# First block's attention logits as three fp32r part products, their maxima bank by bank, and the heads' loads at other tiles

## The reference

```
q = concat(q_nope, rope(q_rope))              # 96 per head
k = concat(k_nope, rope(k_rope))              # the 32 rope columns are shared by all heads
logits = einsum('bqhd,bkhd->bhqk', q, k) * (1 / sqrt(96))
p = softmax(logits, axis=-1)
o = einsum('bhqk,bkhd->bqhd', p, v)
```

## Time and profile before

| | |
|---|---|
| median of 3 runs | 2934.79 us (2934.61 to 2935.14) |
| the profiled execution | 2935.57 us, span 2934.2 us |
| TensorE busy | 2836.1 us (97%) |
| VectorE, ScalarE, GpSimd busy | 1356.9, 1125.4, 1277.9 us |
| heads of c0 | 91.0 to 151.8 us |
| heads of l0 | 288.1 to 406.8 us |
| heads of l1 | 1128.1 to 1246.8 us |
| modulation weights, 512 KB each | 6.5 us from issue to landing (median) |

### The profile page before, as it was taken

One profiled execution on the slowest core, in us unless ns is written; L12 is line 12 of the kernel. 1 busy time (PEld: TensorE's weight loads), 2 busy tenths in 40 slices (PEclk: granted clock), 3 DMA queues, 4 the chain that ended last, 5 costly groups with the idle time before them and its releaser, 6 DMA issues.

```text
span 2934.2 us, 40890 instructions
## 1 busy us (share of the span) xinstructions
PE 2836.1 (97%) x16278; PEld 2341.0 (80%) x16278; DVE 1356.9 (46%) x2527; ACT 1125.4 (38%) x1917; POOL 1277.9 (44%) x828
## 2 busy tenths in 40 slices
PE   7789999999999999989999899999999999999999
PEld 6577778888888786778888787888878878888887
DVE  5448643241211576632211457776542368667432
ACT  4353554553332444543332344332433344323332
POOL 4253247874444442344444353343534433435343
PEclk9899999999999999999999999999999999999999
DMA  7834114653233324033333222111223221212222
GB/s 260 307 106 152 39 49 151 181 160 101 94 94 129 113 82 144 1 108 94 96 93 102 71 97 69 58 58 58 87 72 94 77 89 49 68 58 72 85 73 87
DMA packets 81981, 291.67 MB, mean 99 GB/s; under 512 B 9216, under 2 KB 9600, under 8 KB 81408
## 3 DMA queue, kind: packets, MB, share of 16 engines
q1 hardware_dynamic: 81792, 289.06, 30.6%
HBM read 286.93 MB, written 2.10 MB: 99 GB/s over the span
## 4 chain that ended last, share of the span: by engine, by line
PE 84%; DVE 10%; ACT 2%; issue 2%; POOL 1%; DMA 1%; SPq 0%; POOLq 0%; ACTq 0%; DVEq 0%
PE ps L625 65%; PE ps L598 5%; DVE ps L2263 4%; PE ps L769 3%; PE ps L790 2%; PE ps L958 1%; PE ps L653 1%; PE ps L1021 1%; PE ps L1032 1%; PE ps L894 1%; PE ps L1199 1%; DVE t L2555 1%; DVE t L2593 1%; POOL t L2895 1%; PE ps L907 0%
## 5 line engine op out<-in xcount | busy, mean ns | idle before, releaser
L625 PE MATMUL ps<-t,t 128*128 128x512 f32 (+3 forms) x9936 | 2210.7, 380 | 20.9 <-DVE t L2027 7.4
L625 PEld LDWEIGHTS ps<-t,t 128*128 128x128 f32 x9936 | 1778.5, 189 | 366.5 <-issue 33.1
L2895 POOL TENSOR_TENSOR t<-t,t 128x1024 fp32r<-128x1024 f32 (+3 forms) x444 | 1041.0, 2348 | 1105.4 <-ACT t L1335 1064.9
L1335 ACT ACTIVATE t<-t 128x1024 fp32r<-128x1024 f32 (+3 forms) x444 | 457.9, 1035 | 855.1 <-PE ps L625 806.0
L598 PE MATMUL ps<-t,t 128*128 128x128 f32 (+2 forms) x1662 | 237.5, 279 | 33.9 <-DVE t L2078 12.2
L598 PEld LDWEIGHTS ps<-t,t 128*128 128x128 f32 (+2 forms) x1662 | 190.4, 141 | 80.9 <-ACT t L1448 16.1
L2366 DVE TENSOR_TENSOR ps<-ps,t 128x512 f32<-128x512 f32 (+1 forms) x96 | 57.2, 606 | 344.1 <-ACT t L1641 344.1
L2379 DVE TENSOR_TENSOR t<-ps,t 128x512 f32<-128x512 f32 x60 | 40.9, 692 | 217.6 <-PE ps L625 217.5
L2263 DVE SCALAR_TENSOR_TENSOR ps<-t,t,ps 128x512 f32<-128x512 f32 (+1 forms) x174 | 116.1, 667 | 6.4 <-ACT ps L1556 0.6
L2915 POOL TENSOR_TENSOR t<-t,t 128x4 f32<-128x4 f32 (+2 forms) x93 | 85.6, 921 | 75.3 <-DVE t L2036 39.3
L769 PE MATMUL ps<-t,t 96*128 96x384 f32 (+1 forms) x320 | 105.6, 453 | 4.8 <-DVE t L2126 2.4
(11 more groups left out here) (264 smaller groups left out, 2398.8 us busy)
## 6 DMA issues: line engine op xcount, KB each, us to landing
t<-in_wbig SPq DMA_DIRECT2D x412, 512.0 KB, 3.5
t<-in_wmod SPq DMA_DIRECT2D x96, 512.0 KB, 6.5
t<-in_wbig SPq DMA_DIRECT2D x16, 416.0 KB, 3.2
t<-in_wbig SPq DMA_DIRECT2D x14, 256.0 KB, 2.7
t<-in_wbig SPq DMA_DIRECT2D x8, 332.0 KB, 3.0
t<-in_wbig SPq DMA_DIRECT2D x6, 384.0 KB, 3.1
t<-in_x SPq DMA_DIRECT2D x1, 2048.0 KB, 8.2
out<-t SPq DMA_DIRECT2D x8, 256.0 KB, 2.1
```

The costliest lines, as they stand in the source:

```text
L625: m = p.matmul(out, lhs, rhs, start=kk == 0 and n == 0, stop=kk == tiles - 1 and n == 2)
L1335: a.activation(c.hi(w), c.raw(w), ACT.Copy).then_inc(w_hi.h, w_hi.up(("cut", w)))
L2895: g.tensor_tensor(c.lo(w), c.raw(w), c.hi(w).bitcast(F32), ALU.subtract).then_inc(w_lo.h, w_lo.up(("cut", w)))
```

## The change

Queries and keys of a head are held as a high part (fp32r, written by ScalarE) and a low part (written by VectorE as the difference). The logits are three fp32r products per bank. For the context tokens all 256 keys go to one bank; the latent stages' low parts lie in AH and AL. VectorE takes the maximum of each bank by itself. `load_head` moves from the second to the first tile of a head on TensorE and ScalarE and stays at the second on VectorE; VectorE's `load_rest` moves from the third to the fourth. The output of an odd head is transposed into columns 384:512 of the pair of three tiles on, ahead of that tile's logits, and is read out by VectorE at the start of the next step, after that tile's exponential. The modulation groups of the heads stages stand at other steps, and in the latent stages their weights no longer use AH's columns.

```
-        return {17: 3, 23: 1}.get(n, 4 if n % 2 else 0)
+        return {13: 4, 17: 3, 23: 1}.get(n, 0)
...
+    def head_parts(self, n, h):
+        Q, K, b = self.QT[h % 2], self.KT[h % 2], h % 2
+        if n == "c0":
+            return Q[:, 0:256], Q[:, 256:512], K[:, 0:256], K[:, 256:512]
+        low = self.AL[0:96, 0:3, :].rearrange("p k n -> p (k n)")
+        return Q, self.AH[0:96, b, :], K, low[:, 768 * b:768 * b + 768]
+
+    def turned_back(self, n, u, nt):
+        return self.pair(("u", n, u + 3))[:, 384:512] if u + 3 < NH * nt else self.bank(("ob", n, u))[:, 0:128]
...
 (TensorE)
         def logits(u):
-            P.wait_ge(act, ("qt", n, h))
+            if odd(u - 3, nt):
+                P.wait_ge(dve, ("oc", n, u - 3))
+                turns([Q[:, 384:512]], [turned_out(u - 3)], ("ob", n, u - 3))
+            P.wait_ge(dve, ("ql", n, h))
             P.wait_ge(dve, ("kt", n, h))
-            for j in range(2):
-                k0, kn = j * nh, min(nh, nk * 128 - j * nh)
-                m = p.matmul(Q[:, 512 * j:512 * j + kn], c.QT[b][:, 128 * t:128 * t + 128], c.KT[b][:, k0:k0 + kn],
-                             start=True, stop=True)
-            m.then_inc(product.h, product.up(("lg", n, u)))
+            for j in range(na):
+                for part, (qp, kp) in enumerate(((QH, KH), (QH, KL), (QL, KH))):
+                    m = p.matmul(Q[:, 512 * j:512 * j + nh], qp[:, 128 * t:128 * t + 128],
+                                 kp[:, nh * j:nh * j + nh], start=part == 0, stop=part == 2)
+                m.then_inc(product.h, product.up(("lg", n, u, j), *([("lg", n, u)] if j == na - 1 else [])))
         def turn(u):
             P.wait_ge(act, ("ex", n, u))
+            if odd(u - 3, nt):
+                P.wait_ge(dve, ("o", n, u - 3))
...
-            if odd(u - 3, nt):
+            if u >= n_u and odd(u - 3, nt):
                 back(u - 3)
             if 1 <= u <= n_u:
                 turn(u - 1)
...
-            if u % nt == 1 and u // nt + 1 < NH:
+            next(tail, None)
+            if u % nt == 0 and u // nt + 1 < NH:
                 load_head(u // nt + 1)
                 if nt == 2:
                     load_rest(u // nt + 1)
-            next(tail, None)
...
-    rest = onward(weave(heads("c0"), mods(0, 5, 12, [6, 7]), 0.45, -1.0), 2 * NH + 2)
+    rest = onward(beside(heads("c0"), mods(0, 5, 12, [6, 7]), (2, 4, 6, 8, 10, 12, 14)), 2 * NH + 2)
...
-    rest = onward(beside(heads("l0"), mods(1, 2, 5, [6, 7]), (4, 5, 12)), 4 * NH + 2)
+    rest = onward(beside(heads("l0"), mods(1, 2, 5, [6, 7]), (4, 12, 20)), 4 * NH + 2)
 (ScalarE)
+            a.activation(QH[:, 0:128 * nt], Q[0:96, 0:128 * nt], ACT.Copy).then_inc(act.h, act.up(("qt", n, h)))
+            A.wait_ge(turned, ("kt", n, h, 0))
+            a.activation(KH[0:64, 0:w], Q[0:64, 512:512 + w], ACT.Copy).then_inc(act.h, act.up(("kh", n, h, 0)))
 (VectorE)
-            V.wait_ge(turned, ("kt", n, h, 0))
-            v.tensor_copy(c.KT[h % 2][0:64, 0:w], c.pair(("head", n, h))[0:64, 512:512 + w]).then_inc(
+            V.wait_ge(act, ("qt", n, h))
+            v.tensor_tensor(QL[:, 0:T], Q[0:96, 0:T], QH[:, 0:T].bitcast(F32), ALU.subtract).then_inc(
+                dve.h, dve.up(("ql", n, h)))
+            V.wait_ge(act, ("kh", n, h, 0))
+            v.tensor_tensor(KL[0:64, 0:w], Q[0:64, 512:512 + w], KH[0:64, 0:w].bitcast(F32), ALU.subtract).then_inc(
                 dve.h, dve.up(("ktr", n, h, 0), ("kt", n, h)))
...
-            V.wait_ge(product, ("lg", n, u))
-            v.tensor_reduce(mx, lg, AX.XY, ALU.max).then_inc(dve.h, dve.up(("mx", n, u)))
+            for j, to in enumerate((nm, mx)[2 - na:]):
+                V.wait_ge(product, ("lg", n, u, j))
+                v.tensor_reduce(to, lg[:, j, :], AX.X, ALU.max).then_inc(dve.h, dve.up(("mx", n, u)))
             V.wait_ge(dve, ("mx", n, u))
-            v.tensor_scalar(nm, mx, -SM1, None, ALU.mult).then_inc(dve.h, dve.up(("nm", n, u)))
+            if na == 2:
+                v.tensor_scalar(nm, mx, nm, -SM1, ALU.max, ALU.mult).then_inc(dve.h, dve.up(("nm", n, u)))
...
         def back(u):
+            if u + 3 < NH * nt:
+                V.wait_ge(act, ("ex", n, u + 3))
             V.wait_ge(turned, ("ob", n, u))
...
         for u in range(n_u + 5):
+            if u <= n_u and odd(u - 4, nt):
+                back(u - 4)
             if u < n_u:
                 logits(u)
...
-            if u % nt == 2 and u // nt + 1 < NH:
+            if nt > 2 and u % nt == 3 and u // nt + 1 < NH:
                 load_rest(u // nt + 1)
-            if odd(u - 3, nt):
+            if u >= n_u and odd(u - 3, nt):
                 back(u - 3)
             if 1 <= u <= n_u:
                 turn(u - 1)
```

More of the change, by code:

```diff
@@ L1433, in attention @@
     def attention(n, nk, nt, tail):
+        k0s = list(range(0, nk, 4))
         def load_head(h):
+            QH, QL, KH, KL = c.head_parts(n, h)
+            Q, w = c.pair(("head", n, h)), 128 * min(4, nk)
             A.wait_ge(turned, ("qt", n, h))
@@ L1944, in act_program @@
     run(mods(1, 1, 2))
-    rest = onward(beside(heads("l0"), mods(1, 2, 5), (4, 5, 12)), 4 * NH + 2)
+    rest = onward(beside(heads("l0"), mods(1, 2, 5), (4, 12, 20)), 4 * NH + 2)
     row_of("l0")
@@ L1961, in act_program @@
     run(mods(1, 6, 7))
-    rest = onward(beside(heads("l1"), mods(1, 7, 10), (4, 5, 12)), 4 * NH + 2)
+    rest = onward(beside(heads("l1"), mods(1, 7, 10), (4, 12, 20)), 4 * NH + 2)
     row_of("l1")
@@ L2839, in dve_program @@
     run(steps)
-    rest = onward(weave(heads("c0"), mods(0, 5, 12), 0.45, -1.0), 2 * NH + 2)
+    rest = onward(beside(heads("c0"), mods(0, 5, 12), (2, 4, 6, 8, 10, 12, 14)), 2 * NH + 2)
     next(rest)
```

104 lines of the change are left out of this document (65 added, 39 removed).

## The result

The changed kernel takes 2968.55 us (median of 4 runs, 2965.99 to 2971.16), the kernel before 2934.97 us beside it (2934.61 to 2937.24). The ratio is 1.0112, 95% interval 1.0099 to 1.0125: slower by 33.6 us. The forecast was 2943.8 us with a range up to 2957: right in sign, wrong in size by 25 us.

The account below looks back on a forecast made before the run. TensorE, busy in 97% of the span, was taken as the bound. Two latent stages at +5.5 us gave +11, context heads about -2: +9 on the median 2934.79, so 2943.8 us, range 2925 to 2957.

Parts of the forecast that it names:

- Products: Latent logits: six fp32r products in 1.05 us replace two fp32 in 1.29, minus 7.7 us a stage.
- Maxima: Latent tiles: one maximum per bank shortens the chain from logits to transposes, so old waits go, minus 2.0 us a stage.
- (a): Even head after odd, second tile: TensorE waits 1.2 us for VectorE's output read-out, three times a stage, plus 3.7 us.
- (b): Tile after (a): maxima, scaling, read-out and exponential outlast TensorE's work by 0.8 us, three times a stage, plus 2.4 us.
- First pair: First pair of heads in a latent stage: loads and shared-key copies make the exponential late once, plus 1.5 us.
- (c): Next head's first logits wait 0.8 us for the last low-part subtraction; modulation groups cover three of four, plus 0.8 us.
- (d): Even heads: value products wait for ScalarE's copy of transposed exponentials, queued behind the next exponential, plus 4.9 us a stage.
- (e): Latent stage start: another ScalarE copy and second VectorE pass before first logits, plus 1.4 us; stage end, plus 0.5 us.
- Head loads: Each head needs more ScalarE copies and two VectorE subtractions; TensorE's eight transposes for it stand one tile sooner.
- Rival 3: Waits also cost clock: one 1.2 GHz stretch in each latent stage loses 10 us, 2954 us in all; chance 0.19.
- Context heads: Context tokens' 16 tiles: cheaper products and fewer load waits against read-out waits, about minus 2 us, between -4 and +1.5.
- Rival 4: Logits: fp32r on 96 rows no faster than at 512 columns, stage grows by 10 us, 2960 us; chance 0.03.

Follow-up runs that it names:

- experiment 3: On the changed kernel, ScalarE's copy of the transposed exponentials put ahead of the next tile's exponential in one latent-stage step of eight: 2962.07 us.
- experiment 1: On the changed kernel, the conv tail one step sooner from the sixth step of each latent stage, on all four engines: 2956.29 us.
- experiment 8: The eighth kernel: on Experiment 7's, latent conv tail starts one step later, VectorE's load_rest ahead of valued, two banks' order changed on TensorE: 2933.04 us.
- Experiment 7: On the changed kernel, the edits of experiments 1, 3 and 5 together, plus the bank of a head's rest freed at its own last subtraction: 2939.09 us.
- experiment 11: On experiment 1's kernel, the conv tail's start one step later with the change of the banks' order, without the VectorE swap: 2948.46 us.
- experiment 5: On experiment 1's kernel, VectorE's low parts of every second head one step sooner in the latent stages: 2949.74 us.
- experiment 2: On the changed kernel, VectorE's read-out moved to the end of the step before, ahead of the head's low parts: 2975.7 us.

## Why the prediction was wrong

Point by point, for one latent stage (predicted plus 5.5, measured plus 17.7 and 16.7):

- Products, minus 7.7: mis-sized. Six products of 384 columns on 96 rows take 1.12 us, or 1.24 ahead of value products, not the 1.05 of the line between the two widths in rows 8; 0.15 to 0.17 saved a tile makes 5.1.
- Maxima, minus 2.0: right. Where nothing else stood ahead, the transposes started 1.44 to 1.56 us after the logits in the kernel before, and 1.13 to 1.15 in the changed one, which is the products' own time; over the stage the small waits that the list leaves out sum to 1.7 us before.
- (a) and (b), plus 3.7 and 2.4: right in place and mechanism, a little smaller. 1.00 and 0.63 us three times, 4.9 for 6.1.
- First pair, plus 1.5: 1.2 us of wait for the exponential (L1490), as said.
- (c), plus 0.8: 0.65 (or 0.7) once, the groups of modulation covering the others, as said.
- (d), plus 4.9: 5.9 less the 1.6 of before, 4.3. Shown by experiment 3.
- (e), plus 1.4 at the start: first logits 4.68 us after the first transposes instead of 3.34, plus 1.3. The end, plus 0.5: nothing; from the last logits to the next projection 13.2 us (411.31 to 424.47) against 13.3 before (394.83 to 408.16).
- Memory queue, no cost: right, no wait of TensorE in a latent stage is for a weight.
- The step that failed is "Head loads". It said that TensorE's eight transposes "stand one tile sooner" and priced only the cover that this takes from others. They need two PSUM banks, and the conv tail's transposes, now directly in front of them, had just filled one. The price is ScalarE's queue down to that copy, 6.9 us a stage, more than the whole forecast of the stage. The question to ask of every moved instruction was in my own list for DMAs and queues, and I did not ask it of its output bank. Taken away by experiments 1 and 8.
- The same omission once more: the modulation group takes a bank that is held until two copies are done, 1.8 us. Experiment 7 frees it.
- The clock. Rival 3 said that the waits would also cost clock, going by a wait of 1.9 us that had; I gave it 0.19, since the waits I knew were 1.2 to 1.5. The two that I did not know are 1.8 to 2.0, and both low stretches of a stage of the changed kernel follow one of them, at 4.1 and 3.3 us a stage, near the 5 that the rival had. That a wait near 2 us is the condition does not hold: experiment 11 has a low stretch behind 1.05 and 1.52 us, and experiment 5 none behind 1.77. The Trainium skill ("TensorE: Matmul & The Clock Gate", HAM oscillation) says that a wait that is long enough throttles the clock and that the work behind it starts cold. The traces agree that waits do it, 0.50 behind the wait of 1.97 us, though the waits of the page's example are longer than any here. Rival 3's time (2954) came nearer than the forecast for a partly wrong reason, and is still 15 us short.
- Context heads, minus 2: minus 1.4 in one pair of profiles, which is inside the spread of 285.4 to 289.1 for l0's start, so it is not shown.
- Rival 4's price is mis-added: 0.32 us more a tile than forecast makes 10 us in each of two stages on top of 2943.8, 2964 and not 2960. The forecast does not use it.

With 6.9 and 1.8 in its sum and the products at 5.1, the prediction's own working would have given 5.5 + 8.7 + 2.6 = 16.8 for the stage, which is the 16.7 and 17.7 that were measured. Part of that agreement is luck: the sum's other terms together came out some 2.5 us smaller than forecast, and the clock's 3.3 to 4.1 is not in it. By what was measured the account closes: 20.6 us of listed waits, minus 5.1 for the products, minus 1.7 for the small waits, plus 4.1 and 3.3 for the clock make 17.9 and 17.1, an estimate from the starts, against 17.7 and 16.7. The clock is also why two stages with the same waits differ by 1.0 us.

Of the 33.6 us, the repairs took back 12.3 (three waits for the tail's bank, experiment 1), 6.5 (the copy, 3), 6.5 (low parts, 5), 4.1 (the modulation's bank, by subtraction, 7) and 6.0 (the tail's start, the banks' order and the swap, with their clock, 8): 35.4. The eighth kernel's waits still sum to 11.4 us in the stage against 5.1 in the kernel before, 12.6 more over both stages. Against them stand the products' 9.5 us and the small waits, 1.7 in each stage: that is why the best version only equals the kernel before, 2933.0 against 2934.9 us.

## What to carry to other kernels

Moving an instruction moves its claim on a buffer too: for each one moved, write down which bank it fills, who has it now, and behind what on that engine's queue its release stands. Where two engines' work alternates, put added work in the tiles where the bounding engine is long on something else, not where it is short; the link that is named as the releaser is often only the last of a chain, and moving that link alone (experiment 2) left the wait as long as it was. A gain on the bounding engine counts for less where it waits: the same products were worth 5.8 us in one version and 9.5 in another. And an edit is read best from the stage it touches: stretches that no edit touches differed by up to 5 us from one profile to the next.

## What was not expected of the hardware

- fp32r products of 384 columns with 96 rows start 0.187 us apart (six in 1.12), above the 0.175 that lies between 0.122 for 256 columns and 0.229 for 512. Whether the rows, the turn of weights at each product or the width does it was not tried.
- Much the same waits cost clock at one place and not at another. Behind waits of 1.05, 1.52 and 1.97 us the changed kernel's clock was at 1.2 GHz. In the first latent stage of experiment 11, behind 1.05, 1.52 and 1.71, it stayed at 2.4 GHz; in its second stage it fell behind 1.05 and 1.52. The modulation group's wait of 1.77 us was followed by 1.2 GHz in experiment 1, where one of 1.19 stood ahead of it, and not in experiment 5, where that one was 0.21. Waits of 1.64 us by themselves, three in each stage of the changed kernel, never cost clock; one of 1.63 with one of 0.66 behind it did in experiment 2. Which of a wait's length and its neighbours decides, no run settles.
